# A float32 decoder layer on one core: in the last stage the sums of two of six dense token blocks stay in PSUM, and h comes in parts

## The reference

```python
proj = x @ w_in                                  # then retention and sliding-window attention
h = layer_norm(ALPHA * x + mix, ln1_w, ln1_b)
# PEER: 8 heads, 16 of 16384 experts for each head and token; u_tab, v_tab are 16384 x 1024
a = gelu(einsum('cd,ced->ce', h, u_tab[idx])) * g
ffn = einsum('ce,ced->cd', a, v_tab[idx])
out = layer_norm(ALPHA * h + ffn, ln2_w, ln2_b)
```

## Time and profile before

| | |
|---|---|
| median of 3 runs | 3078.61 us |
| the profiled execution: time | 3082.5 us |
| its span | 3080.7 us |
| its mean granted TensorE clock | 0.985 |
| PE busy | 2980.4 us, 97% |
| DVE busy | 2327.8 us, 76% |
| ACT busy | 1204.8 us, 39% |
| POOL busy | 1053.0 us, 34% |
| DMA | 693.46 MB, mean 225 GB/s |

### The profile page before, as it was taken

One profiled execution on the slowest core, in us unless ns is written; L12 is line 12 of the kernel. 1 busy time (PEld: TensorE's weight loads), 2 busy tenths in 40 slices (PEclk: granted clock), 3 DMA queues, 4 the chain that ended last, 5 costly groups with the idle time before them and its releaser, 6 DMA issues. The chain is left out here.

```text
span 3080.7 us, 42384 instructions
## 1 busy us (share of the span) xinstructions
PE 2980.4 (97%) x15866; PEld 2565.9 (83%) x15866; DVE 2327.8 (76%) x4289; ACT 1204.8 (39%) x2245; POOL 1053.0 (34%) x750
## 2 busy tenths in 40 slices
PE   7997998999999999999999999979999999999998
PEld 6887886888888899989898999868888888888887
DVE  4214775567988888888887556569998998999898
ACT  2112332222222566656566657533333333333331
POOL 3222221001455443443434454424433333333331
PEclk9997998999999999999999999989999999999999
DMA  4223222222677666666666888789988898888881
GB/s 169 84 89 123 104 97 83 72 79 69 236 247 255 228 225 234 223 246 241 240 231 250 288 299 301 290 297 317 321 299 302 283 313 292 295 307 296 298 306 74
DMA packets 291846, 693.46 MB, mean 225 GB/s; under 512 B 20304, under 2 KB 134352, under 8 KB 288464
## 3 DMA queue, kind: packets, MB, share of 16 engines
q1 hardware_dynamic: 189776, 315.61, 30.7%
q0 software_dynamic: 73728, 268.47, 24.4%
q10 hardware_dynamic: 28160, 106.96, 9.0%
HBM read 564.08 MB, written 126.88 MB: 224 GB/s over the span
## 5 line engine op out<-in xcount | busy, mean ns | idle before, releaser
L1443 PE MATMUL y_ps<-v_hi,a_hi 128*128 128x512 f32 x1536 | 600.1, 391 | 20.4 <-DVE y L1572 11.5
L1444 PE MATMUL y_ps<-v_lo,a_hi 128*128 128x512 f32 x1536 | 599.6, 390 | 0.0
L1445 PE MATMUL y_ps<-v_hi,a_lo 128*128 128x512 f32 x1536 | 599.4, 390 | 0.0
L799 POOL TENSOR_TENSOR u_lo<-u_raw,u_hi 128x1024 fp32r<-128x1024 f32 x128 | 314.6, 2458 | 725.0 <-ACT u_hi L795 724.0
L1104 PE MATMUL z_first<-hT_hi,u_hi 128*128 128x512 f32 x1024 | 409.9, 400 | 9.5 <-PEq L825 5.1
L1508 POOL DMA_INDIRECT v_rows<-in_v,room x192 | 259.7, 1353 | 463.1 <-DVE y L1555 439.2
L1106 PE MATMUL z_first<-hT_hi,u_lo 128*128 128x512 f32 x1024 | 401.3, 392 | 0.0
L1105 PE MATMUL z_first<-hT_lo,u_hi 128*128 128x512 f32 x1024 | 400.7, 391 | 0.0
L1443 PEld LDWEIGHTS y_ps<-v_hi,a_hi 128*128 128x128 f32 x1536 | 289.6, 189 | 81.6 <-issue 11.9
L1445 PEld LDWEIGHTS y_ps<-v_hi,a_lo 128*128 128x128 f32 x1536 | 289.6, 189 | 60.4
L1444 PEld LDWEIGHTS y_ps<-v_lo,a_hi 128*128 128x128 f32 x1536 | 289.6, 189 | 60.3
(11 more groups left out here) (195 smaller groups left out, 5829.4 us busy)
## 6 DMA issues: line engine op xcount, KB each, us to landing
u_raw<-in_uT SPq DMA_DIRECT2D x128, 512.0 KB
room<-in_v SPq DMA_DIRECT2D x128, 512.0 KB
z<-z_sb ACTq DMA_DIRECT2D x128, 384.0 KB
gates<-g_sb ACTq DMA_DIRECT2D x24, 2048.0 KB
room<-z SPq DMA_DIRECT2D x16, 1536.0 KB
z_in<-z SPq DMA_DIRECT2D x16, 1536.0 KB
g_in<-gates SPq DMA_DIRECT2D x16, 1536.0 KB
room<-gates SPq DMA_DIRECT2D x15, 1536.0 KB
```

The source lines that it names most:

```text
L799: self.nc.gpsimd.tensor_tensor(self.u_lo[e][:], self.u_raw[e][:], self.u_hi[e][:].bitcast(F32), ALU.subtract).then_inc(self.u_lo_in[e], 1)
L1443: nc.tensor.matmul(o, ah, v_hi[p][:, i, c], start=(i == 0), stop=False)
L1444: nc.tensor.matmul(o, ah, v_lo[p][:, i, c], start=False, stop=False)
L1445: last = nc.tensor.matmul(o, al, v_hi[p][:, i, c], start=False, stop=(i == GROUP - 1))
```

## The change

What it does, by its parts:

1. **Banks.** Blocks 0 and 5 (`HELD`) have two banks each for themselves, and their sums stay there over all 32 rounds; they are added to y once, at the end. Blocks 1 to 4 (`CYCLED`) share the other four banks, two pairs in turn. Rounds take these blocks in alternating order (0 1 2 3 4 5, then 0 4 3 2 1 5), so the last cycled block of a round is the first of the next and goes on in the same banks. A "run" is one stay in a bank pair: 3 runs are closed in a round, where before 6 blocks were. PE waits, ahead of a run, until the run before the last has been read.
2. **Order of making.** The operands of round r are made in the order in which round r-1 consumed (`made(r)`). Round 0 consumes 0 1 2 5 3 4; the first four are again done in two passes.
3. **h.** Four DMAs in place of one: the cycled blocks (2 MB) ahead of round 1's z and gates; the row blocks (1 MB) behind these and ahead of v(1, 0); the two held blocks (0.5 MB each) behind all of v(1). The scaling of the dense blocks is folded into their first addition (scalar_tensor_tensor in place of tensor_tensor). The row blocks are scaled by a 128x2048 instruction at the second place of round 1.
4. **Rows.** `spread` puts the 8 rows of round 1 into its last four places (2 each). In round 31 the row blocks are finished at places 1 and 2 in place of 1 and 3.

```diff
+        HELD = (0, DB - 1)
+        CYCLED = list(range(1, DB - 1))
+        LAST = len(CYCLED) - 1
+        def order(r):
+            if r == 0:
+                return [HELD[0], *CYCLED[:2], HELD[1], *CYCLED[2:]]
+            return [HELD[0], *(CYCLED[::-1] if r % 2 else CYCLED), HELD[1]]
+        def run(r, s):
+            return LAST * r + (LAST - CYCLED.index(s) if r % 2 else CYCLED.index(s))
+        def banks(r, s):
+            first = 2 * HELD.index(s) if s in HELD else 4 + 2 * (run(r, s) % 2)
+            return y_ps[first:first + 2]
+        def opens(r, s):
+            return r == 0 or (s not in HELD and run(r, s) > LAST * r)
+        def closes(r, s):
+            return r == NG - 1 or (s not in HELD and run(r, s) < LAST * (r + 1))
+        def made(r):
+            return order(max(r - 1, 0))
...
-            mine = rows_of(r)
-            return mine[len(mine) * s // DB:len(mine) * (s + 1) // DB]
+            mine, first = rows_of(r), 2 if r == 1 else 0
+            at = [len(mine) * max(k - first, 0) // (DB - first) for k in (s, s + 1)]
+            return mine[at[0]:at[1]]
...
                 load_v(0, first=2)
+                load_h(slice(GB + 1, TB - 1), cycled_here)
                 load_z(1)
-                sp.dma_start(y[:], d["h"].rearrange("n p c -> p n c")).then_inc(h_here, 16)
+                load_h(slice(0, GB), rows_here)
                 load_v(1)
+                load_h(slice(GB, GB + 1), held_here)
+                load_h(slice(TB - 1, TB), held_here)
...
                 for r in range(NG):
-                    for s in range(0 if r else 4, DB):
-                        pe.wait_ge(a_lo_in, DB * r + s + 1)
+                    for s in order(r)[0 if r else 4:]:
+                        pe.wait_ge(a_lo_in, DB * r + made(r).index(s) + 1)
                         for a in range(2):
-                            wait(pe, y_read, BANKS * r + 2 * s + a - 7)
+                            if s not in HELD and opens(r, s):
+                                wait(pe, y_read, 2 * run(r, s) + a - 3)
                             turn(r, s, a, range(GROUP))
...
                 def add(r, s):
+                    held = s in HELD
+                    first = held or r == 0 or (r == 1 and s == CYCLED[-1])
...
+                        if first:
+                            ins = nc.vector.scalar_tensor_tensor(part, part, ALPHA, o, ALU.mult, ALU.add)
+                        else:
+                            ins = nc.vector.tensor_tensor(part, o, part, ALU.add)
+                        ins.then_inc(held_read if held else y_read, 1)
...
-                v.wait_ge(h_here, 16)
-                nc.vector.tensor_scalar(y[:], y[:], ALPHA, None, ALU.mult).then_inc(h_scaled, 1)
-                v.wait_ge(h_scaled, 1)
                 for r in range(1, NG):
-                    for s in range(DB):
+                    for n, s in enumerate(made(r)):
                         if s >= SKIP:
                             product(r, s)
-                        add(r - 1, s)
-                        if s < GROUP:
-                            split_v(r, s)
-                        if s:
-                            lo(r, s - 1)
-                        for i in spread(r, s):
+                        if closes(r - 1, s):
+                            add(r - 1, s)
+                        if n < GROUP:
+                            split_v(r, n)
+                        if n:
+                            lo(r, made(r)[n - 1])
+                        if r == 1 and n == 1:
+                            v.wait_ge(rows_here, 16)
+                            nc.vector.tensor_scalar(y[:, 0:GB], y[:, 0:GB], ALPHA, None, ALU.mult).then_inc(h_scaled, 1)
+                            v.wait_ge(h_scaled, 1)
+                        for i in spread(r, n):
                             add_row(i)
-                        if r == NG - 1 and s % 2 and s // 2 < GB:
+                        if r == NG - 1 and 1 <= n <= GB:
...
-                    lo(r, DB - 1)
-                for s in range(DB):
+                    lo(r, made(r)[-1])
+                for s in order(NG - 1):
                     add(NG - 1, s)
```

More of the change, by code:

```diff
@@ L1395, in spread @@
         def spread(r, s):
-            mine = rows_of(r)
-            return mine[len(mine) * s // DB:len(mine) * (s + 1) // DB]
-        finish_order = list(range(GB)) + list(range(GB, TB))
+            mine, first = rows_of(r), 2 if r == 1 else 0
+            at = [len(mine) * max(k - first, 0) // (DB - first) for k in (s, s + 1)]
+            return mine[at[0]:at[1]]
+        finish_order = list(range(GB)) + [GB + s for s in order(NG - 1)]
         with nc.Block() as block:
@@ L1449, in _ @@
                 for part in (range(GROUP // 2), range(GROUP // 2, GROUP)):
-                    for s in range(4):
+                    for n, s in enumerate(order(0)[:4]):
                         if part[0] == 0:
-                            pe.wait_ge(a_lo_in, s + 1)
+                            pe.wait_ge(a_lo_in, n + 1)
                         for a in range(2):
@@ L1477, in _ @@
                 split_v(0, 0)
-                hi(0, 0)
+                hi(0, made(0)[0])
                 split_v(0, 1)
-                for s in range(1, DB - 1):
+                for s in made(0)[1:4]:
                     hi(0, s)
@@ L1483, in _ @@
                 split_v(0, 3)
-                hi(0, DB - 1)
+                for s in made(0)[4:]:
+                    hi(0, s)
                 nc.scalar.activation(a_rows[:], ahead.z_rows[:, 0:GB], ACT.Gelu).then_inc(rows_gelu, 1)
@@ L1493, in _ @@
                                                  ACT.Gelu).then_inc(gelu_in, 1)
[L1494 to L1498 removed]
+                        if n < GROUP:
+                            split_v(r, n)
+                        if n:
+                            hi(r, made(r)[n - 1])
+                    hi(r, made(r)[-1])
             @block.gpsimd
@@ L1567, in add @@
                 def add(r, s):
+                    held = s in HELD
+                    first = held or r == 0 or (r == 1 and s == CYCLED[-1])
+                    if held:
+                        v.wait_ge(held_here, 32)
+                    elif first:
+                        v.wait_ge(cycled_here, 16)
                     for a in range(2):
-                        n = BANKS * r + 2 * s + a
                         c = slice(a * 512, (a + 1) * 512)
-                        v.wait_ge(y_done, n + 1)
-                        nc.vector.tensor_tensor(y[:, GB + s, c], y_ps[n % 8][:], y[:, GB + s, c], ALU.add).then_inc(
-                            y_read, 1)
+                        part, o = y[:, GB + s, c], banks(r, s)[a][:]
+                        v.wait_ge(y_done, BANKS * r + 2 * order(r).index(s) + a + 1)
+                        if first:
[3 more added lines that the diff above has]
+                        ins.then_inc(held_read if held else y_read, 1)
                 def split_v(r, i):
@@ L1580, in _ @@
                 split_v(0, 0)
-                lo(0, 0)
+                lo(0, made(0)[0])
                 split_v(0, 1)
-                for s in range(1, DB - 1):
+                for s in made(0)[1:4]:
                     lo(0, s)
```

47 lines of the change are left out of this document (28 added, 19 removed).

## The result

The changed kernel is slower by a little: 3086.98 us, the median of 19 runs (3084.4 to 3091.35), beside 3081.63 us for the kernel before in 19 runs (3078.38 to 3085.48). The ratio is 1.0018, with a 95% interval of 1.0011 to 1.0025. That is 5.4 us more, where 0.4 us less was forecast, and 3087 lies outside the range of 3073.5 to 3083.5. (The median of these 19 runs of before lies 3 us above that of the three that the forecast was set against; the ratio is free of that.) Of the experiments' runs two stood far off all the others, one of the kernel before at 8438 us and one of experiment 5 at 7397 us, and are in no ratio.

A forecast was written before the change was run, and what follows sets the result against it. PE's own rate bounds rounds 2 to 31, and 16.9 us are lost at the start. Waits and slow matmuls of 8.0 + 1.5 + 5.3 + 1.7 = 16.5 replace these, so 3078.6 - 0.4 = 3078.2 us, range 3073.5 to 3083.5.

The forecast's parts named there:

- A: Start of DVE's first addition (block 1 of round 0), forecast at 2037.1, waiting for v(1, 0) and no longer for h.
- stall 1: PE's wait in round 0 until DVE's first addition frees a bank: to fall from 11.66 to 8.0 us.
- stall at block 4 of round 1: New PE wait at 2055.8 for lo(1, 4), with rows packed ahead of it on DVE: 5.3 us.
- slow start: First 11 matmuls of the last stage take 4.82 us, not 2.49: 2.33 us lost.
- shared bandwidth: Start of the stage: if transfers shared it, v(1, 0) could come with the gates at 2031, winning 3 us more: 3075.2.
- Stall 2: PE's 1.98 us wait in round 1 for the low part of v(1, 3), forecast to vanish.
- 2 rows: Additions of two gathered rows at each of round 1's places 3 to 6 on DVE, 1.20 us per row.
- the part on the steady rounds: DVE loses 3.6 of 29.3 us of work a round; nothing is won, as PE sets the pace.
- the two cases of the kernel before: Slow matmuls after PE's 11.66 and 1.98 us waits cost 1.53 and 1.72 us; 1.5 and 1.7 were forecast.
- the chain holds no time besides A: DVE's chain up to lo(1, 4): each us on the first addition's start is one us on the end.
- The rival that counted on it: Steady rounds: DVE is late to additions by over 4.6 us, PE waits each round; half a us gives 3093.2; 10%.
- z late and A late: Upper bounds at the start: z(2) late loses 2 us, first addition at 2039.7 loses 2.2; with the end's 1, 3083.4.

The follow-up runs named there:

- experiment 5: Kernel before with h loaded in parts, scaling folded into the first addition, no rows at round 1's first two places: 3074.86 us, ratio 0.998.
- experiment 7: Changed kernel with DVE's additions of blocks 1 and 2 of round 0 ahead of its loop: 3085.31 us, ratio 1.0005 to the kernel before.
- experiment 6: Changed kernel's banks and orders, with one load of h at its old place, scaled ahead of the loop: 3089.53 us, ratio 1.0032 to the kernel before.
- experiment 1: Changed kernel without gathered rows in round 1, the 256 rows spread over rounds 2 to 30: 3076.62 us, ratio 0.9988 to the kernel before.
- 2: Changed kernel with the held blocks' h and the norm's weights loaded behind round 2's v: 3085.69 us, ratio 1.0017 to the kernel before.
- experiment 3: Changed kernel with round 2's z and gates issued only when the fifth row has landed: 3091.14 us, ratio 1.0028 to the kernel before.
- experiment 4: Changed kernel with round 1's rows over all six places and the row blocks' scaling at the first: 3085.86 us, ratio 1.0012 to the kernel before.
- experiment 8: Changed kernel with blocks 1 and 2 of round 0 added ahead of DVE's loop and no rows in round 1: 3075.24 us, ratio 0.9976.
- 9: Kernel before with h in parts, no rows in round 1, round 0's first two additions ahead of DVE's loop: 3070.77 us, ratio 0.9961.
- 10: Kernel before's banks, h in parts, no rows in round 1, round 0's first four additions ahead of DVE's loop: 3070.86 us, ratio 0.9964.

## Why the prediction was wrong, point by point

Most of the prediction's times hold. In us, the arrivals and A taken from the first matmul of the stage:

| | forecast | measured |
|---|---|---|
| z and gates of round 1 at ACT | 24.7 | 24.6 |
| v(1, 0) at ACT | 28.5 | 28.4 |
| first addition, A | 31.3 | 31.2 |
| stall 1 | 8.0 | 8.3 |
| slow matmuls behind it | 1.5 | 2.9 |
| stall for v's low part in round 1 | none | none |
| lo(1, 4) made, from A | 23.85 | 28.4 |
| stall at block 4 of round 1 | 5.3 | 8.4 |
| slow matmuls behind it | 1.7 | 2.8 |
| slow start | 2.3 | 2.0 |
| lost in all | 18.8 | 24.4 |
| z and gates of round 2 at ACT | 58.2 to 61.2 | 58.6 |
| rounds 2 to 31 | no stall | no stall |
| from round 31's second addition to the end of DVE's last instruction | 35.1 | 35.1 |

**The first addition hangs on v and not on h: right.** Experiment 7 takes the addition out of v's shadow, and the stall is gone; 6 brings h back, and it is 14.2. The Trainium skill ("DMA: Bandwidth & Descriptors", Queues, rings and completion order) says that each DMA engine takes its descriptors in ring order. The trace agrees: v(1, 0) came at 28.4 us, where shared bandwidth would have brought it at 25.2 by the prediction's reckoning.

**Stall 2 goes: right**, PE has no stall for a low part of v in the trace after.

**A new wait at block 4, for the rows packed ahead of lo(1, 4): right in its place and its cause** (experiment 1).

**What failed is a term of the sum from A: "2 rows" at 1.20 us each, with no wait for their data.** The chain was summed as if the rows were there. The argument for that stood in the part on the steady rounds: "1.7 us for rows". But that was a figure of the kernel before, where the fifth row's gather went ahead of round 2's z. The change advances z by 7 us and packs the rows; I had worked out the new issue time of z (2042) and used it for z's own landing alone, and never asked what it does to the gathers beside it. The second half of it I had not looked for either: POOL's instruction for the fifth row, 1.14 us before, took 4.08 (the table behind experiment 7). The cost is 4.3 us in the chain, which ends at A + 28.4 and not at A + 23.85. At PE 3.1 us more of idling are seen, as PE itself comes 1.4 us later, by its slow matmuls. Experiments 2, 3 and 4 move these waits by moving z or the rows.

**The other term is the slow matmuls behind a stall:** 1.5 and 1.7 by the two cases of the kernel before, 2.9 and 2.8 measured. Together 2.5 us. That was a range taken for a value: two cases gave no bound, and I kept none.

Stall 1 gives another 0.3, and the slow start 0.3 the other way. The sum of the misses is 5.6, which is what is between 18.8 and 24.4. By the prediction's own rule, that the chain holds no time besides A, this can be put more simply. The slow matmuls behind stall 1 cost nothing: had they been fewer, PE would have waited for lo(1, 4) that much longer. The chain from A is 4.5 us longer, 4.3 of them for the two rows, and the slow matmuls behind the second stall are 1.1 more; these two make the miss, and the rows are four fifths of it.

**The steady rounds: right that they win nothing.** The thinner bank cover did not fail there. The rival that counted on it falls for the kernel as changed; but 3 and 8 show it at one place, in round 2, when DVE comes late by z: 3.1 us each. For that place my sum gave 0.6 to 3.6 us of cover for block 4's first bank. In the changed kernel DVE had read it at 2068.28 and PE wanted it at 2075.68, 7.4 us later. That it held so easily was luck: PE had lost 5.6 us more than forecast by then, and in experiment 8, where that loss is gone, PE waits there.

**The range.** It had z late and A late as its bad cases, 3083.4. With all terms as measured the sum would have been 3078.2 + 5.6 = 3083.8, just past that; the rest to 3087 is the 3 us by which the median of before moved between 3 runs and 19.

## What to carry to other kernels

Work taken off an engine that has been waiting for another is worth nothing in the steady state; look for what it costs at the edges, here an addition that lost its first place and a block whose operands are the last made and the second used. When a change moves a load ahead, write down every other transfer that now finds it on the DMA engines, gathers above all, since the lack of a wait in the old trace is no proof for the new one. When a change takes an instruction out of an engine's order, ask also what used its place: here the held block's place has no addition, and POOL's gather stood behind DVE's work for the length of it. And when one in-order engine feeds another, clearing one wait only moves the time to the end of the chain: PE got 11 us back at the first stall and gave nearly all of it back at the next (experiment 7), until the chain itself was made shorter (1 and 8 to 10).

## What the runs showed of the hardware

The stretch at half clock (granted 0.50 of full speed, 1.2 GHz, and matmuls 0.427 us apart, against 0.227 at 2.4 GHz) after PE had been idle has no fixed length, and does not follow the idle time: 11.5 us of idling and 7 slow matmuls (kernel before), 14.0 and 7 (experiment 6), 8.0 and 8 (2), 8.1 and 14 (after), 8.5 and 13 (1). Its cost is 1.5 to 2.9 us a stall. After an idle time of 1.6 us or less the next matmuls were at full clock or nearly so (2043.05 and 2048.04 above); after 1.8 us in the kernel before nine were slow. After 3.06 and 3.25 us (8 and 5) the first two or three came 0.23 to 0.31 us apart and the slow ones only behind them, with 1.7 us lost in all; after 3.08 us (3) fourteen were slow from the first, with 2.8 us lost.

A gather's instruction on POOL takes 0.94 to 1.15 us in most cases and up to 4.08 us in some, and what lengthens it is what DVE does meanwhile. DVE in the changed kernel beside the fifth row's gather, which runs from 2042.76 to 2046.84:

```profile
2042.40 1.28 DVE L1598 SCALAR_TENSOR_TENSOR y<-v_rows,a_rows,y 128x1024 f32<-128x1024 f32 x1
2043.60 0.69 DVE L1603 TENSOR_TENSOR z_in<-z_in,g_in 128x512 f32<-128x512 f32 x1
2044.20 1.22 DVE L1629 TENSOR_TENSOR v_lo<-room,v_hi 128x1024 fp32r<-128x1024 f32 x1
2045.34 0.68 DVE L1607 TENSOR_TENSOR a_lo<-z_in,a_hi 128x512 fp32r<-128x512 f32 x1
2045.94 2.47 DVE L1598 SCALAR_TENSOR_TENSOR y<-v_rows,a_rows,y 128x1024 f32<-128x1024 f32 x2
```

Product and low parts follow each other without a gap from 2043.60 to 2045.94, and the gather ends 0.90 us behind them. This is place 4, the held block's, where no addition from PSUM stands behind the product. In the kernel before each place has one, and a gather that starts at the same point of the order ends 0.90 us behind the product alone (2055.53):

```profile
2054.09 2.34 POOL L1508 DMA_INDIRECT v_rows<-in_v,room  x1 [3.59 <-DVE y L1555]
```

Of the gathers from 2030 to 3030 us, 501 in the twelve runs take 2.3 us or more; every one of them ends 0.87 to 0.90 us after the end of such an unbroken stretch of DVE's products, low parts and scalings (taken by the start of what follows it). No such end is tied to an addition from PSUM or to an addition of a row. The order of work does not settle it alone: in experiment 7 a gather at the same point took 1.74 us. POOL in order of time in experiment 4, where the first two rows are added singly and the next two as a pair, shows both kinds:

```profile
2038.87 1.14 POOL L1551 DMA_INDIRECT room<-in_v,room  x1 [30.26 <-DVE y L1598]
2043.60 1.14 POOL L1551 DMA_INDIRECT v_rows<-in_v,room  x1 [3.59 <-DVE y L1598]
2048.33 4.08 POOL L1551 DMA_INDIRECT v_rows<-in_v,room  x1 [3.59 <-DVE y L1598]
```

The third gather starts 0.85 us ahead of place 4's stretch (2049.18 to 2051.52). It is 4.08 us with round 2's z held back as well (experiment 3), so it isn't the filled queue of the DMAs. No run changed DVE's order for this alone, so that DVE's stretch is the cause is read from where these gathers end, and not from an experiment.
